# Second block: sine products and index logits left in PSUM, search rounds dealt over other units, pool copies and results put ahead of the index scores, the first two output units run in token halves

## The chip, the cores and the metric

The kernel runs on one core of a Trainium2 chip. The metric is the device time of one execution in microseconds (us), as the median of several runs. One more execution was taken by the hardware profiler; every duration below is from it.

## What is computed

The program runs two layers of a hybrid block (dilated attention, gated delta rule, gated feed-forward), then two layers of a second block. The change is made for the second block. Of one layer of it, with S = 512 tokens and a width of 1024:

```python
h = rms_norm_2(x, g_pre_mix[l])
proj = h @ w_in[l]
u_pool, q, k, v, iq, ik, iw = jnp.split(proj, SPLIT_POINTS, axis=-1)
q, k, iq, ik = (rope_partial(t, positions, 16) for t in (q, k, iq, ik))
# pool_mixer: window means of 2, 4, 8, 16 tokens minus u, times w_pool (4 groups of 128 channels)
a_out = pool_mixer(u_pool, w_pool[l], pool_scale[l])
# dsa_attention: which keys a query may look at
logits = jnp.einsum('bqhd,bsd->bqhs', iqb, ik32) * (IDX_DIM ** -0.5)
score = jnp.einsum('bqh,bqhs->bqs', iwb, jax.nn.relu(logits))     # 8 index heads
top_val, top_idx = lax.top_k(score, topk)                         # topk = 128
# softmax attention over the chosen keys, 8 heads of 64
b_out = dsa_attention(q, k, v, iq, ik, iw, topk)
mix = jnp.concatenate([a_out, b_out], axis=-1) @ w_out[l]
x = x + rms_norm_2(mix, g_post_mix[l])
f = jnp.square(jax.nn.relu(rms_norm_2(x, g_pre_ffn[l]) @ w_ff1[l])) @ w_ff2[l]
x = x + rms_norm_2(f, g_post_ffn[l])
```

## The kernel before, in words

Activations lie channel by token: a tile has 128 channels on the partitions and 512 tokens along the free axis. A **unit** is one tile of 128 output channels of a projection. TensorE (PE) makes it with 8 steps over the 1024 input channels (`unit`, L1869), and each step is three matmuls, because weights and activations are split into a high and a low fp32r part: high by high, low weight by high, high by low activation. For each unit SyncE loads 512 KB of weights (`load`, L705), ScalarE (ACT) makes the high part (`w_high`, L945), GpSimd (POOL) the low part by a subtraction (`w_low`, L761). Units alternate between two PSUM accumulators; a unit may start when the unit two before it has been copied out (`acc_free`).

Nothing is scheduled at run time. Each engine has its own list of instructions, written out in the order of the Python loops, and engines meet at semaphores; an engine whose next instruction waits holds up everything behind it. In the second block the loop over `u` from 0 to 21 gives that order for all engines:

- Units 0 to 4 are the index key and the index queries; 5 to 8 the four pool groups; 9 to 17 (without 11) queries and keys; 18 to 21 the values. "Unit" 11 (`WPOOL`) is the pool's own small product (`pool_mix`, L2045 to L2047).
- For rotated units ACT copies the accumulator to `turn2_in` (`turn_input`, L1032), PE multiplies by a permutation (`turn`, L2008) into `SC[j % 2]`, VectorE (DVE) multiplies by the sine (L1427), POOL multiplies the copy by the cosine (L901), DVE adds the two (L1431). `j` counts the turned units. The values are transposed instead (L2012), and DVE scales them out of PSUM into `v` (L1435).
- The pool units are scaled by DVE into `pu` (`unit_scaled`, L1416); this copy is what frees the accumulator. `pool_window` then adds shifted copies of `pu` (L1780, L1781), 1, 2, 3 or 4 times for g = 0 to 3, forms the mean minus `pu` (L1785 to L1789), and ACT and POOL split it (L986, L797). `pool_scaled` (L1768) reads the result of the small product from PSUM.
- The index logits are 16 **pairs** of matmuls (`index_logits`, L2000; two heads each, 128 to 512 keys wide), put between the last steps of units 6 to 10 and 12 by the table `IX_AT`. They alternate between two pairs of PSUM banks. ACT applies the ReLU into one of four SBUF buffers `ir` (L1261), DVE adds them up with the head's weight into `bias` (`index_score`, L1726, L1728).
- The search for the 128th largest score is 16 rounds for each of three query tiles (tile 1, 2 and 3, with 256, 384 and 512 keys). A round takes the 8 largest (L1742) and strikes them out (L1745); at the end of a tile `bias` becomes a mask (L1750). `TOP_AT` gives the rounds of each `u`, `TOP_STEPS` those that run within the attention.

Two places in DVE's loop over `u` set what follows (before):

```python
for y in (2 * pair + h for pair in IX_AT.get(u + 1, ()) for h in range(2)):
    index_score(w, y)
j = turn_of(1, u)
if j is not None:
    turn_finish(w, j)
elif u != WPOOL:
    pool_window(w, u - POOL_U)      # begins with unit_scaled
```

The attention (`attention`) has 35 slots; slot n makes scores (L2099), which DVE adds to `bias` (L1449), ACT exponentiates (L1041), PE transposes (L2111) and multiplies by `v` (L2124). Between them PE runs the 32 steps of the first half of the output product, whose input is the pool's result (`half_step` with `second` 0, L2069 to L2071). The second half needs the attention's result. It comes in four pieces of 128 tokens; each goes through ACT (L1056), DVE (L1467), ACT (L986) and POOL (L797) before PE may read it. After slot 34 PE runs 8 output units of 4 steps of 3 matmuls (`half_step` with `second` 1, the same lines).

## Time and profile before

| | us |
|---|---|
| median of 3 runs | 2866.94 |
| lowest, highest | 2864.83, 2867.55 |
| the profiled execution | 2872.96 |
| its span, first to last instruction | 2871.2 |
| PE busy in it | 2730.1 (95%) |
| second block, first layer: first unit to the end of the output product | 1554 to 1830 |
| the same of its second layer | 2214 to 2486 |

Times inside the span are counted from its start. "PE" rows are matmuls; their ends are modelled and overlap, so the distance from one start to the next is what a matmul costs. Numbers in square brackets behind a row are the idle time of the engine just before it, and who ended it. The granted clock of a stretch is 1.00 at 2.4 GHz and 0.50 at 1.2 GHz.

### The profile page before, as it was taken

To read this page: it belongs to the slowest core of one execution; us is meant where nothing else is said; L and a number is where in the kernel's file an instruction comes from. 1 tells how busy PE (TensorE), PEld (TensorE's weight loads), DVE (VectorE), ACT (ScalarE), POOL (GpSimd) and SP (SyncE) were. 2 spreads that over 40 slices of the span, in tenths; PEclk is the share of its full clock that TensorE was granted. 3 is DMA by queue.
4 is the path that set the end of the run, shared out by engine and by line. 5 is a ranking of instruction groups with operands and counts; after the bars stand their busy time and mean duration, and the time that the engine had idled before them with its cause. 6 is when DMAs were issued, how large, how long until landed. Compare 5 with 4: busy or idle time off the path is not lost.

```text
span 2871.2 us, 43482 instructions
## 1 busy us (share of the span) xinstructions
PE 2730.1 (95%) x15240; PEld 2153.9 (75%) x15240; DVE 1138.9 (40%) x2246; ACT 1111.2 (39%) x1846; POOL 1221.4 (43%) x630
## 2 busy tenths in 40 slices
PE   9998999999999989999999888899999898899997
PEld 7767778888776777788887566788887575688886
DVE  4555445440255553544303774410113675510012
ACT  4454244443335533444423325432323234542331
POOL 3313135554432222355544351364653451264553
PEclk9999999999999999999999999999999999999998
DMA  3211022222221101222232120122222121122222
GB/s 136 76 45 38 9 67 95 95 100 100 101 76 59 52 17 31 77 98 95 95 106 80 66 74 23 52 102 95 95 95 79 64 74 38 52 88 95 96 95 94
DMA packets 62871, 217.22 MB, mean 76 GB/s; under 512 B 6576, under 2 KB 6704, under 8 KB 62480
## 3 DMA queue, kind: packets, MB, share of 16 engines
q1 hardware_dynamic: 62416, 214.28, 21.9%
q8 instruction: 87, 1.43, 0.2%
q0 software_dynamic: 320, 1.12, 0.2%
q14 instruction: 48, 0.39, 0.0%
HBM read 213.28 MB, written 2.10 MB: 75 GB/s over the span
## 4 chain that ended last, share of the span: by engine, by line
PE 85%; DVE 7%; ACT 3%; issue 2%; DVEq 1%; POOL 1%; ACTq 0%; POOLq 0%
PE bank L1869 59%; PE bank L1919 3%; PE bank L2217 3%; PE bank L2069 2%; PE bank L2071 2%; PE bank L2070 2%; PE bank L1931 2%; PE bank L2124 1%; PE bank L2099 1%; PE bank L2111 1%; PE bank L2008 1%; POOL wL L761 1%; PE bank L2034 1%; PE bank L1896 1%; DVE bias L1728 1%
## 5 line engine op out<-in xcount | busy, mean ns | idle before, releaser
L761 POOL TENSOR_TENSOR wL<-raw,wH 128x1024 fp32r<-128x1024 f32 x371 | 903.3, 2435 | 1187.8 <-ACT wH L945 1187.5
L1869 PE MATMUL bank<-hH,wH 128*128 128x512 f32 x1680 | 688.9, 410 | 24.4 <-DVE pu L1416 16.3
L1869 PE MATMUL bank<-hH,wL 128*128 128x512 f32 x1680 | 658.9, 392 | 0.0
L1869 PE MATMUL bank<-hL,wH 128*128 128x512 f32 x1680 | 658.7, 392 | 0.0
L945 ACT ACTIVATE wH<-raw 128x1024 fp32r<-128x1024 f32 x371 | 392.1, 1057 | 519.2 <-PE bank L1869 489.4
L1869 PEld LDWEIGHTS bank<-hH,wH 128*128 128x128 f32 x1680 | 317.8, 189 | 124.1 <-issue 30.4
L1869 PEld LDWEIGHTS bank<-hH,wL 128*128 128x128 f32 x1680 | 318.3, 189 | 69.9 <-issue 9.8
L1869 PEld LDWEIGHTS bank<-hL,wH 128*128 128x128 f32 x1680 | 317.6, 189 | 67.9
L1869 PE MATMUL bank<-hidH,wH 128*128 128x512 f32 x864 | 337.3, 390 | 0.0
L1869 PE MATMUL bank<-hidH,wL 128*128 128x512 f32 x864 | 336.6, 390 | 0.0
L1869 PE MATMUL bank<-hidL,wH 128*128 128x512 f32 x864 | 336.6, 390 | 0.0
L1827 DVE SCALAR_TENSOR_TENSOR relu<-bank,rstd 128x512 f32<-128x512 f32 x64 | 44.1, 691 | 458.8 <-PE bank L1869 449.6
L1869 PEld LDWEIGHTS bank<-hidH,wH 128*128 128x128 f32 x864 | 162.2, 188 | 36.0 <-issue 1.6
L1869 PEld LDWEIGHTS bank<-hidL,wH 128*128 128x128 f32 x864 | 162.3, 188 | 33.8
L1869 PEld LDWEIGHTS bank<-hidH,wL 128*128 128x128 f32 x864 | 162.3, 188 | 32.9
L797 POOL TENSOR_TENSOR hidL<-piece,hidH 128x512 f32 (+1 forms) x108 | 139.8, 1295 | 99.4 <-ACT hidH L986 81.7
L1698 DVE SCALAR_TENSOR_TENSOR mT<-bank,par,mT 128x511 f32<-128x511 f32 (+1 forms) x176 | 131.9, 750 | 117.3 <-ACT mT L1223 103.2
L1041 ACT ACTIVATE sc<-sc,st 128x128 f32<-128x128 f32 (+3 forms) x128 | 71.7, 561 | 139.1 <-DVEq L1452 138.8
L1694 DVE TENSOR_TENSOR bank<-bank,rstd 128x512 f32<-128x512 f32 x88 | 61.5, 699 | 117.9 <-PE bank L1869 110.0
L2069 PE MATMUL bank<-hH,wH 128*128 128x512 f32 x192 | 78.8, 410 | 8.6 <-POOL hL L797 7.0
L990 ACT ACTIVATE sq<-mT 128x512 f32<-128x512 f32 x48 | 30.3, 632 | 131.0 <-DVE mT L1841 76.1
L1369 DVE TENSOR_TENSOR rstd<-rstd,sq 128x512 f32<-128x512 f32 x20 | 17.1, 855 | 150.3 <-ACT sq L990 150.3
(362 smaller groups left out, 3822.9 us busy)
## 6 DMA issues: line engine op xcount, KB each, us to landing
raw<-w_dram SPq DMA_DIRECT2D x398, 512.0 KB, 3.3
x<-x_dram SPq DMA_DIRECT2D x4, 512.0 KB, 9.4
out_dram<-x SPq DMA_DIRECT2D x1, 2048.0 KB, 6.2
const<-const_dram SPq DMA_DIRECT2D x1, 1229.0 KB, 12.8
par_next<-par_dram POOLq DMA_DIRECT2D x5, 168.0 KB, 3.6
qkT<-pos_dram POOLq DMA_DIRECT2D x1, 256.0 KB, 7.1
const<-const_dram SPq DMA_DIRECT2D x1, 131.0 KB, 2.2
```

Of the source, the lines that this page charges most:

```text
L761: pool.tensor_tensor(wL[:, s, :], raw[:, s, :], wH[:, s, :].bitcast(F32), ALU.subtract).then_inc(w_lo.sem, 1)
L797: pool.tensor_tensor(dst, shape(src), hi.bitcast(F32), ALU.subtract).then_inc(piece_lo.sem, 1)
L945: act.activation(wH[:, s, :], raw[:, s, :], ACT.Copy).then_inc(w_hi.sem, 1)
L1041: act.activation(sc[:, n % 2, 0:wd], sc[:, n % 2, 0:wd], ACT.Exp, bias=st[:, MN + n % 4:MN + n % 4 + 1], scale=-1.0, accum_out=st[:, SUM + ...
L1694: dve.tensor_tensor(banks[s][:, :], banks[s][:, :], rstd[:, :], ALU.mult).then_inc(acc_scaled.sem, 1)
L1698: last = dve.scalar_tensor_tensor(buf[:, lag:S], banks[s][:, 0:S - lag], prmd(w, "fconv", i * 12 + 6 * q + 3 * s + 2 - lag), buf[:, lag:S] ...
L1869: mm = pe.matmul((out or ACC[bk])[:, :], wt[:, c:c + P], rhs, start=first and k == 0 and j == 0, stop=last and k == tiles - 1 and j == 2)
L1919: pe.matmul(out[u][:, :], wt[:, k * P:k * P + P], hH[:, k, :], start=k == 0 and j == 0, stop=False)
L1931: mm = pe.matmul(out[u][:, :], three[u][0][:, k * P:k * P + P], hL[:, k, :], start=False, stop=k == KD - 1)
L2069: pe.matmul(out[:, :], wH[:, p % 2, c:c + P], high, start=k == 0, stop=False)
L2070: pe.matmul(out[:, :], wL[:, p % 2, c:c + P], high, start=False, stop=False)
L2217: mm = pe.matmul(o, *two, start=True, stop=True)
```

## The change

- `turn_finish`: the product with the sine is written back into the PSUM bank it was read from, in both blocks; the addition then reads PSUM and SBUF.
- `index_score` reads the logits from PSUM, where ACT's ReLU now leaves them. `ix_used` (DVE has read them) takes the place of `ix_relu` (ACT has copied them) in the waits of `index_logits` and `pool_mix`; the buffers `ir` and ACT's wait for them go.
- The last shifted addition of `pool_window` goes to the PSUM bank `SC[1]`; turn 5, the next to use that bank, waits until the fourth window is done.
- In DVE's loop `unit_scaled` and, at `WPOOL`, `pool_scaled` stand ahead of the index scores.
- The rounds are dealt anew: at `u` = 10 one for tiles 1 and 2; at 11 two for all three; at 12 to 20 one for all three, with one more for tile 1 at 13 to 16 and one more for tile 2 at 18 to 20; none at 21. Tile 2's last round runs in slot 1, five of tile 3 in slots 3 to 11 (six before).
- The last two transposes of values go to the banks `OA` and `TRO`, and slot 0 waits for turns 0 to 14 alone; slot 4 waits for all 17.
- The output units 0 and 1 of the second half run in two parts, tokens 0 to 255 and 256 to 511. The first part waits for two of the four attention pieces, the second for all.

```diff
@@ -184,16 +184,18 @@
 assert _y == 16
 
 
-TOP_AT, TOP_STEPS, _r, _r3 = {}, {}, 0, 0
-for _u in range(10, IN2):
-    _n, _n3 = 1 + (_u >= 18), int(_u >= 12)
-    TOP_AT[_u] = [[(1, r), (2, r)] + [(3, q) for q in range(_r3, _r3 + _n3)][r - _r:r - _r + 1]
-                  for r in range(_r, _r + _n)]
-    _r += _n
-    _r3 += _n3
-assert _r == TOPK // 8
-for _i, _q in enumerate(range(_r3, TOPK // 8)):
-    TOP_STEPS[2 * _i + 1] = [(3, _q)]
+TOP_AT = {10: [[1, 2]], 11: [[1, 2, 3], [1, 2, 3]]}
+for _u in range(12, IN2 - 1):
+    TOP_AT[_u] = [[1, 2, 3]] + ([[1]] if 13 <= _u < 17 else [[2]] if _u >= 18 else [])
+TOP_STEPS = {1: [[2]], 3: [[3]], 5: [[3]], 7: [[3]], 9: [[3]], 11: [[3]]}
+_done = {1: 0, 2: 0, 3: 0}
+for _table in (TOP_AT, TOP_STEPS):
+    for _u in sorted(_table):
+        for _c, _tiles in enumerate(_table[_u]):
+            _table[_u][_c] = [(i, _done[i] + _tiles[:n].count(i)) for n, i in enumerate(_tiles)]
+            for _i in _tiles:
+                _done[_i] += 1
+assert set(_done.values()) == {TOPK // 8}
 
 
 FILL, _f = [], 0
@@ -420,6 +422,10 @@
 
         SIDE = (bank[5], bank[6])
 
+        def turned_bank(b, j):
+
+            return (OA, TRO)[j - 15] if b and j >= 15 else SC[j % 2]
+
         def cst(name, a=0, b=None):
             o, n = CAT[name]
             return const[:, o + a:o + (n if b is None else b)]
...
@@ -1257,8 +1263,7 @@
                     for y in (2 * pair + h for pair in IX_AT.get(u, ()) for h in range(2)):
                         wd = P * (y // 8 + 1)
                         act.wait_ge(ix_done.sem, ix_done.at(w, y + 1))
-                        act.wait_ge(ix_used.sem, ix_used.at(w, y - 3))
-                        act.activation(ir[:, y % 4, 0:wd], index_bank(y)[:, 0:wd], ACT.Relu,
+                        act.activation(index_bank(y)[:, 0:wd], index_bank(y)[:, 0:wd], ACT.Relu,
                                        scale=HD ** -0.5).then_inc(ix_relu.sem, 1)
                     j = turn_of(1, u)
                     if j is not None:
@@ -1417,14 +1422,15 @@
 
             def turn_finish(w, j):
 
-                t1, t2 = ATT[w.b][3][:, 0, :], ATT[w.b][3][:, 1, :]
+                t2 = ATT[w.b][3][:, 1, :]
                 cos, sin = rope_r(w.b)
                 dve.wait_ge(turned.sem, turned.at(w, j + 1))
                 if j < N_ROT[w.b]:
                     if w.b:
                         t2 = pt2[:, j % 2, :]
                         dve.wait_ge(cos_done.sem, cos_done.at(w, j + 1))
-                    dve.tensor_tensor(t1, SC[j % 2][:, :], sin, ALU.mult)
+                    t1 = SC[j % 2][:, :]
+                    dve.tensor_tensor(t1, t1, sin, ALU.mult)
                     if w.b == 0:
                         dve.tensor_tensor(t2, turn_src(w.b, j), cos, ALU.mult)
                     dve.drain()
...
@@ -1720,7 +1726,7 @@
             def index_score(w, y):
 
                 i, h = y // 8, y % 8
-                score, r = bias_of(1, i), ir[:, y % 4, 0:P * (i + 1)]
+                score, r = bias_of(1, i), index_bank(y)[:, 0:P * (i + 1)]
                 dve.wait_ge(ix_relu.sem, ix_relu.at(w, y + 1))
                 if h == 0:
                     dve.tensor_scalar(score, r, iw[:, i, 0:1], None, ALU.mult).then_inc(ix_used.sem, 1)
@@ -1772,11 +1778,9 @@
 
                 win = 2 << g
                 u = pu[:, g % 2, :]
-                unit_scaled(w, POOL_U + g, u, acc_free[(POOL_U + g) % 2].sem)
-                dve.drain()
                 src = u
                 for step in range(g + 1):
-                    lag, dst = 1 << step, sc2[:, step % 2, :]
+                    lag, dst = 1 << step, sc2[:, step % 2, :] if step < g else SC[1][:, :]
                     dve.tensor_tensor(dst[:, lag:S], src[:, lag:S], src[:, 0:S - lag], ALU.add)
                     dve.tensor_copy(dst[:, 0:lag], src[:, 0:lag])
                     dve.drain()
@@ -1798,22 +1802,28 @@
                         copy_gates(w)
                     if u == 2:
                         gate_scale(w)
+                    j = turn_of(1, u)
+                    if j is None and u != WPOOL:
+                        unit_scaled(w, u, pu[:, (u - POOL_U) % 2, :], acc_free[u % 2].sem)
+                        dve.drain()
+                    if u == WPOOL:
+                        for g in (0, 1):
+                            pool_scaled(w, g)
                     for y in (2 * pair + h for pair in IX_AT.get(u + 1, ()) for h in range(2)):
                         index_score(w, y)
-                    j = turn_of(1, u)
                     if j is not None:
                         turn_finish(w, j)
                     elif u != WPOOL:
                         pool_window(w, u - POOL_U)
-                    if u in (WPOOL, WPOOL + 1):
-                        for g in (0, 1) if u == WPOOL else (2, 3):
+                    if u == WPOOL + 1:
+                        for g in (2, 3):
                             pool_scaled(w, g)
                     for rounds in TOP_AT.get(u, ()):
                         top_round(rounds)
                 for n in range(SLOTS):
                     attention(w, n)
-                    if n in TOP_STEPS:
-                        top_round(TOP_STEPS[n])
+                    for rounds in TOP_STEPS.get(n, ()):
+                        top_round(rounds)
                 sum_output(w, 0, lambda h: add_half(w, h))
                 residual(w, 0, "post", (w, 1))
                 dve.wait_ge(rstd_ready.sem, rstd_ready.at(w, 2))
@@ -1993,7 +2003,7 @@
                 if pair == 0:
                     pe.wait_ge(turn_done.sem, turn_done.at(w, 5))
                 if pair >= 2:
-                    pe.wait_ge(ix_relu.sem, ix_relu.at(w, 2 * pair - 2 * (pair < 15)))
+                    pe.wait_ge(ix_used.sem, ix_used.at(w, 2 * pair - 2 * (pair < 15)))
                 i = pair // 4
                 for y in (2 * pair, 2 * pair + 1):
                     p0, f = y % 2 * HD, y % 8 // 2
@@ -2001,15 +2011,19 @@
                               ikT[p0:p0 + HD, 0:P * (i + 1)], start=True, stop=True).then_inc(ix_done.sem, 1)
 
             def turn(w, j):
-                src = turn_src(w.b, j)
+                src, to = turn_src(w.b, j), turned_bank(w.b, j)
                 bk, a = acc_of(w, unit_of_turn(w.b, j))
                 pe.wait_ge(acc_free[bk].sem, acc_free[bk].at(w, a + 1))
+                if w.b and j == POOL_U:
+                    pe.wait_ge(piece_ready.sem, piece_ready.at(w, N_PD2 + 4))
+                if w.b and j == 15:
+                    pe.wait_ge(ix_used.sem, ix_used.at(w, 32))
                 if j < N_ROT[w.b]:
-                    pe.matmul(SC[j % 2][:, :], cst("turn2" if w.b else "turn1"), src, start=True,
+                    pe.matmul(to[:, :], cst("turn2" if w.b else "turn1"), src, start=True,
                               stop=True).then_inc(turned.sem, 1)
                 else:
                     for t in range(NT):
-                        tr = pe.transpose(SC[j % 2][:, t * P:t * P + P], src[:, t * P:t * P + P], ident)
+                        tr = pe.transpose(to[:, t * P:t * P + P], src[:, t * P:t * P + P], ident)
                     tr.then_inc(turned.sem, 1)
 
             def narrow(w):
...
@@ -2047,7 +2061,7 @@
                 pe.matmul(MIX[g % 2][:, :], pwH[:, c:c + P], pdL[:, g, :], start=False,
                           stop=True).then_inc(unit_done.sem if g == 1 else pool_done.sem, 1)
 
-            def half_step(w, h, k, second):
+            def half_step(w, h, k, second, part=None):
 
                 p, (bk, a) = HALF_OF[w.b][second] + h // 2, half_at(w.b, h, second)
                 out = half_bank(w.b, h, second)
@@ -2057,7 +2071,8 @@
                     pe.wait_ge(acc_free[bk].sem, acc_free[bk].at(w, a))
                 if h == 0 and w.b:
                     if k == 0:
-                        pe.wait_ge(piece_lo.sem, piece_lo.at(w, (N_ATT2 if second else N_PY2) + 4))
+                        pieces = (N_ATT2 if second else N_PY2) + (4 if part is None else 2 + 2 * part)
+                        pe.wait_ge(piece_lo.sem, piece_lo.at(w, pieces))
                 elif h == 0 and k == 0:
                     pe.wait_ge(piece_lo.sem, piece_lo.at(w, N_DN1 + NT if second else N_ATT1 + 4))
                 c = h % 2 * 512 + k * P
@@ -2066,10 +2081,11 @@
                 else:
                     r = k + 4 * second
                     high, low = hH[:, r, :], hL[:, r, :]
-                pe.matmul(out[:, :], wH[:, p % 2, c:c + P], high, start=k == 0, stop=False)
-                pe.matmul(out[:, :], wL[:, p % 2, c:c + P], high, start=False, stop=False)
-                mm = pe.matmul(out[:, :], wH[:, p % 2, c:c + P], low, start=False, stop=k == 3)
-                if k == 3:
+                cols = slice(0, S) if part is None else slice(S // 2 * part, S // 2 * part + S // 2)
+                pe.matmul(out[:, cols], wH[:, p % 2, c:c + P], high[:, cols], start=k == 0, stop=False)
+                pe.matmul(out[:, cols], wL[:, p % 2, c:c + P], high[:, cols], start=False, stop=False)
+                mm = pe.matmul(out[:, cols], wH[:, p % 2, c:c + P], low[:, cols], start=False, stop=k == 3)
+                if k == 3 and part != 0:
                     mm.then_inc(unit_done.sem if h % 2 else half_done.sem, 1)
 
             def gate_step(w, h, k):
@@ -2091,7 +2107,9 @@
                 pt = PTS[w.b]
 
                 if n == 0:
-                    pe.wait_ge(turn_done.sem, turn_done.at(w, (12, 17)[w.b]))
+                    pe.wait_ge(turn_done.sem, turn_done.at(w, (12, 15)[w.b]))
+                if n == 4 and w.b:
+                    pe.wait_ge(turn_done.sem, turn_done.at(w, 17))
                 if n < 32 and n % 2 == 0:
                     pe.wait_ge(sc_read.sem, sc_read.at(w, n))
                     f, i, _ = att_step(n)
@@ -2348,7 +2366,11 @@
                     attention(w, n, FILL[n])
                     if n < 16:
                         keep_warm(STAT, 1)
-                for h in range(KD):
+                for part in range(2):
+                    for h in range(2):
+                        for k in range(4):
+                            half_step(w, h, k, 1, part)
+                for h in range(2, KD):
                     for k in range(4):
                         half_step(w, h, k, 1)
                 output_sum(w, 0)
```

DVE, units 5 to 7 of a layer of the second block (in the middle of the loop over `u`); `pu` is the scaled pool unit, `bias` the scores, `sc` an SBUF buffer, `bank` any PSUM bank. Before:

```order
L1726 TENSOR_SCALAR bias<-ir,iw 128x128
L1728 SCALAR_TENSOR_TENSOR bias<-ir,iw,bias 128x128 x3
L1416 TENSOR_TENSOR pu<-bank,rstd 128x512
L1780 TENSOR_TENSOR sc<-pu 128x511
L1781 COPY sc<-pu 128x1
L1785 TENSOR_TENSOR sc<-sc,const 128x2
L1787 SCALAR_TENSOR_TENSOR piece<-sc,pu 128x512
L1789 TENSOR_TENSOR piece<-sc,pu 128x2
L1728 SCALAR_TENSOR_TENSOR bias<-ir,iw,bias 128x128 x4
```

and now:

```order
L1421 TENSOR_TENSOR pu<-bank,rstd 128x512
L1732 TENSOR_SCALAR bias<-bank,iw 128x128
L1734 SCALAR_TENSOR_TENSOR bias<-bank,iw,bias 128x128 x3
L1784 TENSOR_TENSOR bank<-pu 128x511
L1785 COPY bank<-pu 128x1
L1789 TENSOR_TENSOR sc<-bank,const 128x2
L1791 SCALAR_TENSOR_TENSOR piece<-bank,pu 128x512
L1793 TENSOR_TENSOR piece<-sc,pu 128x2
L1421 TENSOR_TENSOR pu<-bank,rstd 128x512
L1734 SCALAR_TENSOR_TENSOR bias<-bank,iw,bias 128x128 x4
```

The copy that frees the accumulator moved ahead of the scores, and most two-operand instructions now read one operand from a bank.

DVE, from the values of unit 20 to the first attention slot. Before:

```order
L1435 TENSOR_TENSOR v<-bank,rtok 128x4x128
L1742 MAX top<-bias 128x8 x3
L1745 MATCH_REPLACE bias<-top,bias 128x256
L1745 MATCH_REPLACE bias<-top,bias 128x384
L1745 MATCH_REPLACE bias<-top,bias 128x512
L1742 MAX top<-bias 128x8 x2
L1745 MATCH_REPLACE bias<-top,bias 128x256
L1745 MATCH_REPLACE bias<-top,bias 128x384
L1750 TENSOR_SCALAR bias<-bias 128x256
L1752 MEMSET bias 64x64
L1750 TENSOR_SCALAR bias<-bias 128x384
L1752 MEMSET bias 64x64
```

(the last `v` and the rounds of `u` = 21; those of `u` = 20 are the same without the masks), and now from the values of unit 20:

```order
L1441 TENSOR_TENSOR v<-bank,rtok 128x4x128
L1748 MAX top<-bias 128x8 x3
L1751 MATCH_REPLACE bias<-top,bias 128x256
L1751 MATCH_REPLACE bias<-top,bias 128x384
L1751 MATCH_REPLACE bias<-top,bias 128x512
L1756 TENSOR_SCALAR bias<-bias 128x256
L1758 MEMSET bias 64x64
L1748 MAX top<-bias 128x8
L1751 MATCH_REPLACE bias<-top,bias 128x384
L1441 TENSOR_TENSOR v<-bank,rtok 128x4x128
L1454 MEMSET st 128x1
L1455 ISA sc,st<-bank,bias 128x128
```

The last values are followed by the first slot directly; rounds remain only behind the values of unit 20.

PE, where the attention ends and the second half of the output product begins. Before:

```order
L2131 MATMUL bank<-const,st 64x128 x2
L2069 MATMUL bank<-hH,wH 128x512
L2070 MATMUL bank<-hH,wL 128x512
L2071 MATMUL bank<-hL,wH 128x512
L2069 MATMUL bank<-hH,wH 128x512
```

and now:

```order
L2149 MATMUL bank<-const,st 64x128 x2
L2085 MATMUL bank<-hH,wH 128x256
L2086 MATMUL bank<-hH,wL 128x256
L2087 MATMUL bank<-hL,wH 128x256
L2085 MATMUL bank<-hH,wH 128x256
```

24 matmuls of 512 columns became 48 of 256; the order of units 2 to 7 is as it was.

## Rows read from the trace of the kernel before

**Rows 1.** The profile's page: busy time, and the chain that ended last, by engine.
```profile
PE 2730.1 (95%) x15240; PEld 2153.9 (75%) x15240; DVE 1138.9 (40%) x2246; ACT 1111.2 (39%) x1846; POOL 1221.4 (43%) x630
...
PE 85%; DVE 7%; ACT 3%; issue 2%; DVEq 1%; POOL 1%; ACTq 0%; POOLq 0%
```
**Rows 2.** PE's waits, 1560 to 1840: us in total, times, longest.
```profile
PE bank L1869 <- DVE pu L1416: 8.6, 4, 3.9
PE bank L2099 <- DVE v L1435: 6.0, 1, 6.0
PE bank L2069 <- POOL hL L797: 3.5, 1, 3.5
...
PE bank L2045 <- DVE piece L1768: 2.6, 1, 2.6
PE bank L1869 <- POOL wL L761: 1.0, 1, 1.0
```
**Rows 3.** The same waits in the second layer, 2220 to 2500.
```profile
PE bank L1869 <- DVE pu L1416: 7.7, 4, 2.5
```
**Rows 4.** Stages, 1602 to 1812: PE, PEld, DVE, ACT, POOL busy, granted clock, DMA share, GB/s.
```profile
1604.00:1608.00 4.00, 3.50 (x9) 2.77 (x10) 3.76 (x7) 0.00 (x0) 2.19 (x1) 0.57 0.16 54
1806.00:1809.00 3.00, 2.81 (x7) 2.23 (x8) 0.00 (x0) 0.10 (x1) 0.14 (x1) 0.50 0.00 0
```
**Rows 5.** DVE and POOL in order of time, around 1604: start, us.
```profile
1603.76 0.69 DVE L1416 TENSOR_TENSOR pu<-bank,rstd 128x512 f32<-128x512 f32 x1
1604.54 2.20 DVE L1780 TENSOR_TENSOR sc<-pu 128x511 f32<-128x511 f32 x1
1603.83 2.36 POOL L761 TENSOR_TENSOR wL<-raw,wH 128x1024 fp32r<-128x1024 f32 x1 [3.20 <-ACT wH L945]
```
**Rows 6.** DVE by line and shape, 1565 to 1830: busy us, mean ns.
```profile
L1431 DVE TENSOR_TENSOR kT<-sc,pt 128x512 f32<-128x512 f32 x4 | 2.8, 692 | 0.3
L1427 DVE TENSOR_TENSOR sc<-bank,rope_r 128x512 f32<-128x512 f32 x13 | 9.0, 692 | 26.3 <-PE bank L2008 24.7 <-POOL pt L901 1.2 <-issue 0.3
```
**Rows 7.** Index logits, ReLUs and scores: PE, ACT and DVE in order of time.
```profile
1635.47 1.13 PE L2000 MATMUL bank<-ikT,iqT 64*128 64x512 f32 x4
...
1637.42 1.13 PE L2000 MATMUL bank<-ikT,iqT 64*128 64x512 f32 x4
1638.58 1.08 ACT L1261 ACTIVATE ir<-bank 128x512 f32<-128x512 f32 x2 [0.87 <-PE bank L2000]
1639.21 1.59 DVE L1728 SCALAR_TENSOR_TENSOR bias<-ir,iw,bias 128x512 f32<-128x512 f32 x2 [0.62 <-ACT ir L1261]
```
**Rows 8.** The fourth pool window, DVE in order of time.
```profile
1628.81 0.80 DVE L1780 TENSOR_TENSOR sc<-pu 128x511 f32<-128x511 f32 x1
...
1633.12 0.18 DVE L1789 TENSOR_TENSOR piece<-sc,pu 128x16 f32<-128x16 f32 x1
```
**Rows 9.** The turn from projection to attention: DVE and PE in order of time.
```profile
1713.89 0.69 DVE L1435 TENSOR_TENSOR v<-bank,rtok 128x512 f32<-128x512 f32 x1
...
1717.80 0.89 DVE L1742 MAX8 top<-bias 128x8 f32<-128x256 f32 x2
...
1719.85 0.69 DVE L1435 TENSOR_TENSOR v<-bank,rtok 128x512 f32<-128x512 f32 x1
1728.05 0.48 PE L2111 MATMUL bank<-const,sc 128*128 128x128 f32 x1 [2.98 <-ACT sc L1041]
```
**Rows 10.** The end of the attention: PE in order of time, and the chain at 1561.
```profile
1802.31 0.40 PE L2131 MATMUL bank<-const,st 128*64 128x128 f32 x4
1806.19 0.80 PE L2069 MATMUL bank<-hH,wH 128*128 128x512 f32 x1 [3.48 <-POOL hL L797]
1813.16 0.39 PE L2069 MATMUL bank<-hH,wH 128*128 128x512 f32 x1
...
1815.20 0.39 PE L2069 MATMUL bank<-hH,wH 128*128 128x512 f32 x1
...
1561.61 0.89 PE bank L1903 x8
```

8 lines of the change are left out of this document (4 added, 4 removed).

## The prediction

> **What bounds the kernel now.** The page comes first: PE is busy for 95% of the span, and the chain that ended last lies on PE for 85% and on DVE for 7% [rows 1]. The matmuls stay the same but for the last units, so only two things can be won: PE's idle time, and matmuls that run at half the granted clock. The waits of PE, stage by stage, give the first. In the first of the two layers PE waits four times, 8.6 us in all, for `unit_scaled` to free an accumulator, 6.0 for the last values before the attention, 3.5 for the low part of the attention's result, 2.6 for `pool_scaled` and 1.0 for weights [rows 2]. The second layer loses 7.7 instead of 8.6 in the first place [rows 3] and the same elsewhere. The table of stretches gives the second: behind a long wait the granted clock is mostly 0.5 and comes back some 3 us later (0.57 as a mean over 4 us at 1604, 0.50 over 3 us at 1806) [rows 4]. At half clock for 3.2 us, PE does what takes 1.6 us, so such a stretch costs 1.6. The first layer has three in the index and pool stage, after the second and the fourth wait for `unit_scaled` and after that for `pool_scaled`; the second layer has two.
>
> Index and pool stage before, waits and cold stretches: 8.6 + 2.6 + 1.0 + 3 x 1.6 = 17.0 in the first layer, 7.7 + 3.6 + 2 x 1.6 = 14.5 in the second.
>
> **Part 1: operands in PSUM.** The rows in order of time show why DVE is late. `unit_scaled`, from a bank, took 0.69 beside POOL's `w_low`, but the window's first addition, with both operands in SBUF, took 2.20, until POOL's 2.36 us subtraction was over (1603.83 + 2.36 = 1606.19; DVE ended at 1606.74) [rows 5]. With one operand in a bank the length is 0.69 with or without POOL: L1427 has 692 ns over 13 of them, equal to the 692 of L1431's `kT`, which reads SBUF twice and was not blocked [rows 6]. So `turn_finish`'s addition and the window's end are no longer held up (1.5 us at most each). I cost the edits themselves at nothing on DVE, since 692 = 692. **A rule against it:** the Trainium skill, "VectorE: DVE Perf Modes", section on the trn2 errata, gives an instruction a fixed part of 120 cycles with PSUM against 58 in SBUF. By that some 60 instructions per layer would be 0.065 us longer each, an estimate from that page of 3.9 us of DVE a layer, of which at most half would lie on a path: 3.9 us later in the two layers, 2841.5 in place of the 2837.6 below. The trace doesn't bear it out, as the equal means have just shown.
>
> **Part 2: results first, and the wait moved to `ix_used`.** Now `unit_scaled` and `pool_scaled` are ahead of the scores, so the waits of 8.6 and 2.6 in their old form go, but for what DVE has still to finish of the window before, which ends in time in every unit (below). But the logits stay in their bank until DVE has read them. ACT ends two ReLUs of 512 in 1.08, DVE two scores in 1.59 and 0.62 behind the first ReLU, so a pair is free 2.2 after it was made; pairs stand 1.95 apart [rows 7]. Two pairs are in flight, so this alone does not stop PE. What stops it is the window: the scores of unit u's pairs stand in DVE's list behind the window of unit u - 2. The fourth window takes 4.5 (1628.81 to 1633.30) [rows 8], 6.0 if POOL holds it up once as in [rows 5]; an addition and a copy less take 0.84 less. The third pair of a unit wants the first one's bank some 5.5 us after the third pair of the unit before; window and scores together need 4.5 to 6.0 + 0.6 + 1.6 = 6.7 to 8.2. That is a wait of 1.2 to 2.7 in unit 10; I take 2.3, nearer to the blocked end since POOL is busy in most of each unit, 2.1 in unit 9 and 1.2 in unit 8, whose windows and logits are shorter. Units 6 and 7 have windows of one step or none before them: nothing. `pool_mix` now waits until pair 13 is read (0.5 more than its weights, 0.6 kept), and pair 15 in unit 12, the only one that waits for its direct predecessor, waits for the two scores of pair 14: 1.9. Queued behind every such wait on PE is the rest of the unit; ACT and POOL then wait for PE, not PE for them. Sum: 1.2 + 2.1 + 2.3 + 0.5 + 0.6 + 1.9 = 8.6 us idle. Cold stretches: the waits are shorter than those of 3.9 and 2.6 which had one, about as long as the 1.9 at 1604.5 which had one, so I count two, 3.2 us. After: 11.8. **Gain: 17.0 - 11.8 = 5.2 in the first layer, 14.5 - 11.8 = 2.7 in the second, 7.9 in all.** Bounds: 0 (nothing but the place of the waits changes) and 23 (no third pair waits, `pool_mix` 1.1 and pair 15 1.9 stay, one cold stretch: 4.6 a layer, 12.4 + 9.9 = 22.3).
>
> Turn 5's new wait for the fourth window is a few us behind: that window now ends near the end of unit 10, turn 5 comes in unit 12's place. Nothing. The dealing of rounds up to u = 19 fills DVE to at most 5.96 - 2.05 + 1.2 = 5.1 us [rows 9] of PE's 24 x 0.2275 = 5.46 us a unit, so it costs nothing while DVE is not behind.
>
> **Part 3: the turn to the attention.** Before, the values of unit 20 began at 1713.89, those of unit 21 at 1719.85, and the first transposition of probabilities on PE at 1728.05, 8.20 later; a round for tiles 1 and 2 took 2.05 (1717.80 to 1719.85) [rows 9]. Now turns 15 and 16 go to other banks, so PE makes both at once and goes on to slot 0. DVE has between the two `v`: one round of three tiles, the mask of tile 1, a round of tile 2. That is 5.96 - 2.05 + 1.2 + 0.4 = 5.5, the 1.2 being the larger part of 2.05. But of the 8.20 behind the second `v`, all rounds go (5.96 - 0.6 = 5.35) and the mask of tile 1 (0.4) too. Net: 1713.89 + 5.5 + (8.20 - 5.35 - 0.4) = 1721.85, against 1728.05; 0.5 of this is tile 2's mask, which moves to slot 1: 1721.35. **Gain 6.7 a layer.** Late next: DVE's mask and round of tile 2 in slot 1, whose 1.7 us ACT and PE cover with slots and filling steps of the first half. Bounds: 5.5 if DVE is 1.2 late at unit 20, with 5.1 of 5.46 us a unit taken; 8 if slot 0 overlaps better. PE's clock is low in the first attention slots in both cases; nothing counted.
>
> **Part 4: the token halves.** PE ends the attention's last products at 1802.31 + 0.4, waits 3.48 for the low part and starts at 1806.19, at half clock until 1809; the first two units, 24 matmuls, last until 1813.16, 6.97 us, where 24 at the full rate of 0.2275 are 5.5 [rows 10]; the rate is 2.04 for the 9 from 1813.16 to 1815.20. Two of the four pieces have long been there (the query tiles take eight slots each, one tile after another, and a piece is one tile), so 24 half matmuls fill the wait, and 24 more remain behind it; the last two pieces are needed only then. The weights of these units are on the chip before (the wait names the pieces alone). The price of a matmul of 256 columns is not in the trace. Lower bound 0.111, which is 0.89/8 of L1903 with 128-column operands, close to half of 0.2275; upper bound 0.2275, if the weight load, 128x128 as before, sets it. I take 0.12, as PE runs on the columns and L1903's 0.111 contains a load each: 2.9 us in the wait, and 2.9 behind 1806.19 in place of 6.97, as the clock has no wait in front. **Gain 4.0 a layer.** With 0.2275: 24 in 5.5 from 1802.7 end 2.0 after the low part came, then 5.5 more: 1813.7, a loss of 0.6.
>
> **Sum.** 7.9 + 2 x 6.7 + 2 x 4.0 = 29.3, and -1 to 1 for the first block, where PE doesn't wait for `turn_finish`: nothing. The profiled execution would go from 2872.96 to 2843.7; the median of the runs is 6.0 below it, so 2866.9 - 29.3 = **2837.6**.
>
> **Rivals.** (a) *The waits only change place* in the index stage: 7.9 less, 2845.5. For: each third pair can wait, and DVE is busy 3.76 of 4 us there [rows 4]. Against: 8.6 and 2.6 had two causes, order and blocking, and both go. 15%. (b) *Half matmuls cost a full one*: 9.2 less, 2846.8. For: PE loads 128x128 weights for each. Against: L1903. 15%. (c) *The third pairs hardly wait*, because DVE is ahead where it was behind: 22.3 instead of 7.9, 2823.2. 12%. (d) *Slower:* a score that reads a bank and `bias` is itself blocked by POOL, 1.5 us (2.20 - 0.69) [rows 5] on each of the 14 pairs that wait: 21 us idle a layer, and with PE idle a third of the time 10 us of low clock; 31 + 3 in place of 15.8 (mean of the layers) is 18.2 lost, 10.7 gained in parts 3 and 4, 7.5 us a layer slower: 2881.9. It decides when the index stage loses over 10.7 a layer. Against it: L1427 at 692 ns reads SBUF and a bank beside POOL. 3%.
>
> **Chances.** The forecast 52%, (a) 15, (b) 15, (c) 12, (d) 3, (a) and (b) together 3 (2854.7). A measurement of this kernel can tell 0.2%, 5.7 us. Faster in all cases but (d) and a part of (a) with (b) and the lower bound of part 3 (2 x 1.2 more): faster 0.94, same 0.03, slower 0.03. The range goes from (c) to (a) with (b): 2822 to 2855.
>
> **What would show it.** Right: PE's waits for `pu` L1416 gone, new ones at the logits with `bias` as releaser, in units 8 to 10 and before pair 15, 1 to 2.5 us each; L1431's `qT` and `iqT` at 0.69 also beside POOL; L1780's last step likewise; the first probabilities' transposition about 8 us after unit 21; half matmuls 0.12 apart with no wait of 3.5. Wrong: DVE instructions from banks above 0.75 us; waits at the logits above 3 us; half matmuls 0.2 apart or a clock of 0.5 between them; rounds that run into slot 0.

## The result, and the profile after

| | before | changed |
|---|---|---|
| median of 4 runs, us | 2867.24 | 2833.45 |
| lowest, highest | 2864.83, 2867.61 | 2831.67, 2836.53 |
| ratio, 95% interval | | 0.9883 [0.9871, 0.9895] |
| the profiled execution | 2872.96 | 2831.67 |

The change takes 33.8 us off; 29.3 were forecast. The profiled executions lie 41.3 apart, since that of before is 6 above its median and that of the changed kernel 2 below its own. So the traces overstate the gain by some 8 us.

Both layers were cut into four stages. The cuts are rows of PE in order of time: the first logits; the first turn behind the second half of the pool's small product; the first transposition of probabilities; the start of the attention's last products with `st`; the first matmul of the output's square sum. Sums of both layers, us:

| kernel | index | to attention | attention | output | all four |
|---|---|---|---|---|---|
| before | 142.9 | 129.3 | 147.2 | 54.9 | 474.3 |
| changed | 126.6 | 115.6 | 144.3 | 48.6 | 435.1 |
| difference | 16.3 | 13.7 | 2.9 | 6.3 | 39.2 |

The page of the changed kernel, as in [rows 1]: PE is busy 16.6 us less with the same columns to multiply, which fits the granted clock (0.984 in the mean of the execution against 0.978: fewer columns run at half clock), and DVE's part of the chain is a point smaller.

```profile
PE 2713.5 (96%) x15288; PEld 2145.6 (76%) x15288; DVE 1106.0 (39%) x2246; ACT 1109.7 (39%) x1846; POOL 1211.0 (43%) x630
...
PE 86%; DVE 6%; ACT 3%; issue 2%; DVEq 2%; POOL 1%; DMA 0%; ACTq 0%; SPq 0%; POOLq 0%
```

PE's waits, changed kernel, 1555 to 1822 (us in total, times, longest), then the second layer, 2195 to 2470; they answer to [rows 2, 3]:

```profile
PE bank L2010 <- DVE bias L1734: 6.1, 4, 2.0
PE bank L2129 <- ACT sc L1047: 3.6, 1, 3.6
...
PE bank L2059 <- DVE bias L1734: 1.2, 1, 1.2
...
PE bank L2085 <- POOL hL L803: 0.4, 1, 0.4
```
```profile
PE bank L2010 <- DVE bias L1734: 7.4, 4, 2.8
```

The waits for `pu`, for `piece`, for `v` and of 3.5 for `hL` are gone. In their place PE waits at the logits (L2010), for DVE to have read a pair.

Stretches of the changed kernel, columns as in [rows 4]: after the short wait at 1607.5, after that of 2.04 at 1618.1, after the 3.56 before the first transposition, and the token halves.

```profile
1605.00:1609.00 4.00, 3.03 (x16) 1.76 (x16) 3.25 (x8) 2.37 (x7) 1.27 (x1) 1.00 0.36 123
1618.00:1622.00 4.00, 3.93 (x11) 2.56 (x12) 3.25 (x7) 1.97 (x4) 0.00 (x0) 0.58 0.00 0
1711.00:1714.00 3.00, 3.00 (x12) 2.16 (x11) 2.04 (x9) 0.91 (x5) 0.00 (x0) 0.50 0.00 0
1782.00:1788.00 6.00, 5.57 (x52) 5.19 (x49) 0.86 (x2) 2.51 (x3) 1.28 (x1) 1.00 0.29 86
```

The stage with the halves, PE in order of time, answers to [rows 10]. The last product of the attention at 1782.19 is followed by half matmuls at once; they start 0.12 apart, the last of the first part at 1785.37, and the wait for the last pieces is 0.43. The granted clock is 1.00 over the whole stretch.

```profile
1782.19 0.39 PE L2149 MATMUL bank<-const,st 128*64 128x128 f32 x4
1782.51 0.39 PE L2085 MATMUL bank<-hH,wH 128*128 128x256 f32 x1
...
1785.25 0.28 PE L2086 MATMUL bank<-hH,wL 128*128 128x256 f32 x1
1785.37 0.28 PE L2087 MATMUL bank<-hL,wH 128*128 128x256 f32 x1
1786.09 0.39 PE L2085 MATMUL bank<-hH,wH 128*128 128x256 f32 x1 [0.43 <-POOL hL L803]
```

DVE by line and shape answers to [rows 6]: first a row of before (1565 to 1830), then the changed kernel's (1560 to 1800).

```profile
L1431 DVE TENSOR_TENSOR iqT<-sc,pt 128x512 f32<-128x512 f32 x4 | 8.0, 2001 | 0.3
```
```profile
L1433 DVE TENSOR_TENSOR bank<-bank,rope_r 128x512 f32<-128x512 f32 x13 | 9.1, 700 | 18.7 <-PE bank L2022 16.0 <-POOL pt L907 1.9 <-issue 0.3
L1437 DVE TENSOR_TENSOR iqT<-bank,pt 128x512 f32<-128x512 f32 x4 | 2.8, 692 | 0.3
L1784 DVE TENSOR_TENSOR bank<-sc 128x510 f32<-128x510 f32 x1 | 2.7, 2668 | 0.1
```

The addition behind the sine product of the index queries went from 2.0 us in the mean to 692 ns. The window's last step is not protected by its result in PSUM: that of the second window still reads SBUF twice, and took 2.67 beside a subtraction of POOL that ran from 1601.34 to 1603.73.

### The profile page after: what moved, and what is told of

Its sections match the earlier page's. It is cut to its first block, busy times and chain, and to the rows that moved or that the text cites. A ratio compares the mean times of both kernels' runs of the same rounds, so it can differ in the third digit from the quotient of the medians.

```text
span 2829.9 us, 43533 instructions
## 1 busy us (share of the span) xinstructions
PE 2713.5 (96%) x15288; PEld 2145.6 (76%) x15288; DVE 1106.0 (39%) x2246; ACT 1109.7 (39%) x1846; POOL 1211.0 (43%) x630
## 4 chain that ended last, share of the span: by engine, by line
PE 86%; DVE 6%; ACT 3%; issue 2%; DVEq 2%; POOL 1%; DMA 0%; ACTq 0%; SPq 0%; POOLq 0%
PE bank L1879 60%; PE bank L1929 3%; PE bank L2235 3%; PE bank L2085 2%; PE bank L2087 2%; PE bank L2086 2%; PE bank L1941 2%; PE bank L2142 1%; PE bank L2117 1%; PE bank L2129 1%; PE bank L2022 1%; POOL wL L767 1%; PE bank L2048 1%; PE bank L1906 1%; PE bank L1913 1%
## 5 line engine op out<-in xcount | busy, mean ns | idle before, releaser
L1879 PE MATMUL bank<-hH,wH 128*128 128x512 f32 x1680 | 685.0, 408 | 6.1 <-POOL wL L767 6.0
L803 POOL TENSOR_TENSOR hidL<-piece,hidH 128x512 f32 (+1 forms) x108 | 139.9, 1296 | 100.6 <-ACT hidH L992 81.6
L2085 PE MATMUL bank<-hH,wH 128*128 128x512 f32 (+1 forms) x208 | 81.0, 389 | 2.5 <-POOL wL L767 1.4
L2086 PE MATMUL bank<-hH,wL 128*128 128x512 f32 (+1 forms) x208 | 77.8, 374 | 0.0
```

The costliest lines, as they stand in the source:

```text
L803: pool.tensor_tensor(dst, shape(src), hi.bitcast(F32), ALU.subtract).then_inc(piece_lo.sem, 1)
L1879: mm = pe.matmul((out or ACC[bk])[:, :], wt[:, c:c + P], rhs, start=first and k == 0 and j == 0, stop=last and k == tiles - 1 and j == 2)
L2085: pe.matmul(out[:, cols], wH[:, p % 2, c:c + P], high[:, cols], start=k == 0, stop=False)
L2086: pe.matmul(out[:, cols], wL[:, p % 2, c:c + P], high[:, cols], start=False, stop=False)
```

## The experiments

Eleven kernels ran, each beside the kernel before. The table has the stages, both layers together, from one profile each. In these stages a stretch at half clock is 3.41 us long in every profile, or twice that, so one more or less moves an entry by 1.7 us. The last column is the median of before minus that of the kernel, by runs on the same chip; of the changed kernel it is 33.8. The expectations name times as on the chip of the result, where the kernel before took 2867.24. On the chips of the experiments it took 2869.22 (e1 to e4), 2871.18 (e5 to e8) and 2871.14 (e9 to e11), so the gain decides and not the time. The 95% intervals reach 0.0016 to 0.0022 to either side of the ratio, 5 to 6 us.

| kernel | index | to attention | attention | output | all four | gain |
|---|---|---|---|---|---|---|
| e1 no halves | 125.8 | 115.6 | 144.5 | 56.6 | 442.5 | 27.5 |
| e2 old rounds and banks | 127.7 | 129.3 | 142.9 | 48.4 | 448.3 | 21.7 |
| e3 order only | 127.0 | 129.3 | 144.6 | 58.0 | 458.9 | 14.1 |
| e4 operands, order undone | 139.9 | 115.6 | 148.5 | 48.6 | 452.7 | 16.8 |
| e5 no PSUM operands | 127.0 | 118.4 | 146.4 | 48.5 | 440.2 | 33.8 |
| e6 window first | 132.0 | 115.6 | 145.7 | 48.5 | 441.9 | 33.7 |
| e7 that, logits in SBUF | 115.0 | 115.6 | 144.3 | 48.7 | 423.6 | 49.6 |
| e8 new rounds, old banks | 127.0 | 123.8 | 141.4 | 48.4 | 440.7 | 32.4 |
| e9 split late | 130.9 | 115.6 | 142.9 | 48.4 | 437.8 | 35.6 |
| e10 that, logits in SBUF | 123.8 | 115.6 | 147.2 | 48.6 | 435.1 | 36.2 |
| e11 e7, rounds in slots | 116.6 | 108.2 | 142.7 | 48.4 | 415.9 | 56.6 |

**e1, the token halves alone undone.**

```diff
-                for part in range(2):
-                    for h in range(2):
-                        for k in range(4):
-                            half_step(w, h, k, 1, part)
-                for h in range(2, KD):
+                for h in range(KD):
```

> The changed kernel without the token halves: output units 0 and 1 of the second half run whole, behind the wait for all four pieces. Theory (the halves fill PE's 3.5 us wait and keep the granted clock up): the wait of 3.5 us for the low part comes back in both layers, 2.4 us a layer with the clock at full behind it and 4.0 where it falls to half: 5 to 8 us more than the changed kernel, about 2840. Rival (PE's gain at this place came from the clock in one execution only): no difference that can be measured, 2833 to 2836.

2841.71, ratio 0.9901 [0.9885, 0.9918]: 6.3 less gain, as the theory has it. Its output stage is 8.0 longer in the trace, and the waits of its first layer hold the row of before again:

```profile
PE bank L2085 <- POOL hL L803: 3.5, 1, 3.5
```

In the traces the halves are worth 4.0 us a layer where the clock would fall behind the wait, 2.4 where it would not, as in the second layer of before.

**e2, rounds and banks of before.** `TOP_AT`, `TOP_STEPS`, `turned_bank` and slot 0's wait as before.

> The changed kernel with the search rounds dealt as before, the last two values' transposes in the banks of before, and slot 0 behind all 17 turns. Theory (the turn to the attention is the rounds that stand between unit 20 and slot 0 on DVE): PE's 6 us wait before slot 0 comes back, 6.8 us a layer, 2847. Rival (the index stage leaves DVE ahead now, and rounds would be done anyway): under 6 us in all, below 2839.

2847.51, ratio 0.9925 [0.9908, 0.9941]: 12.1 less gain. The stage to the attention is 129.3, to a tenth that of before, and 13.7 above the changed kernel: 6.9 a layer. The attention behind it is 1.4 shorter in both layers together, so the net is nearer to the 12.1 of the medians.

**e3, the order alone, on the kernel before.** (`pool_window` no longer begins with `unit_scaled`, and `pool_scaled` of the first two groups isn't called behind the scores.)

```diff
+                    j = turn_of(1, u)
+                    if j is None and u != WPOOL:
+                        unit_scaled(w, u, pu[:, (u - POOL_U) % 2, :], acc_free[u % 2].sem)
+                        dve.drain()
+                    if u == WPOOL:
+                        for g in (0, 1):
+                            pool_scaled(w, g)
                     for y in (2 * pair + h for pair in IX_AT.get(u + 1, ()) for h in range(2)):
                         index_score(w, y)
```

> The kernel before with one edit: unit_scaled and pool_scaled stand ahead of the index scores in DVE's list; operands, logits buffers, rounds, banks and halves as before. Theory (order and bank operands are both needed): the copies that free accumulators come at once, but the windows are still blocked by POOL beside them and the ReLUs wait for one of four SBUF buffers, so 3 to 5 of the 8 us a layer come: 2857 to 2861. Rival 1 (the order gives the whole of the index stage): 16 us, 2851 or less, with no wait over 1 us left there. Rival 2 (the operands give it): 2865 to 2868.

2855.08, ratio 0.9951 [0.9935, 0.9968]. The gain of 14.1 lies between my theory (6 to 10) and rival 1 (16), nearer to the rival, and the index stage decides for it: 127.0 against 126.6 of the changed kernel, with every operand where it was before. (The output stage, which this edit doesn't touch, is 3.1 longer than before: its second layer had 6.8 us at half clock, where before had none.) The rival's "no wait over 1 us" was wrong; PE waits at the logits here too, for ACT (first layer):

```profile
PE bank L2004 <- ACT ir L1261: 6.0, 4, 2.7
```

**e4, the changed kernel with that order undone.** The same edit backwards.

> The changed kernel with one edit undone: unit_scaled and pool_scaled stand behind the index scores again. Theory (both are needed): PE waits for pu again, 1 to 2 us in four places, and at the logits: 6 us a layer more than the changed kernel, about 2845. Rival 1 (the order gives the whole): 8 us a layer more, 2850. Rival 2 (the operands give it): within 3 us of the changed kernel, 2834 to 2836.

2852.43, ratio 0.9941 [0.9924, 0.9957]: 17.0 less gain, as rival 1 has it. The index stage is 139.9, 3.0 below before. PE waits for DVE again (first layer):

```profile
PE bank L1875 <- DVE pu L1421: 6.0, 4, 1.8
...
PE bank L2055 <- DVE piece L1774: 2.6, 1, 2.6
PE bank L2006 <- DVE bias L1734: 2.0, 2, 1.4
```

So of the 16.3 us the order gives 15.9 alone; all the rest of the change gives 3.0 without it and 0.4 beside it. Even the 3.0 is hardly the operands' own: PE's waits in the stage are only 0.9 shorter than before in both layers together (23.3 against 24.2), and the stage has two stretches at half clock fewer. No run parts the order into its two halves, `unit_scaled` and `pool_scaled`.

**e5, no PSUM operands in the changed kernel.**

> The changed kernel without its PSUM operands: sine product, last window step and the ReLU's logits go to SBUF as before, with the four buffers and their waits; order, rounds, banks of the last values and halves as in the change. Theory after the last runs (the order alone shortens the index stage, operands nothing): as the changed kernel within 2 us, 2832 to 2836, index stage 63 to 64 us. Rival (bank operands save DVE the time that POOL blocks it, and this shows once the rest is in place): 3 to 6 us more, 2837 to 2840, with waits for weights or for DVE that the changed kernel lacks.

2837.36, ratio 0.9887 [0.9869, 0.9906], against 0.9883 of the change: the same gain, 33.8, though the time by itself would fall into the rival's range. The trace shows one place that the rival foresaw, small: the stage to the attention is 1.4 a layer longer. DVE's four additions for `qT` take 1208 ns in the mean here, 692 in the change, it has no idle time to speak of in front of the values (0.3 us instead of 2.7), and slot 0 comes later (PE waits 4.82 instead of 3.56 before the first transposition):

```profile
1713.91 0.48 PE L2129 MATMUL bank<-const,sc 128*128 128x128 f32 x1 [4.82 <-ACT sc L1047]
```

**e6 and e7, the window first.** In DVE's list a unit's window now follows `unit_scaled`, ahead of the next unit's scores; e7 also has the ReLU write to the four buffers `ir`, with the waits of before.

```diff
+                    if j is None and u != WPOOL:
+                        pool_window(w, u - POOL_U)
                     for y in (2 * pair + h for pair in IX_AT.get(u + 1, ()) for h in range(2)):
                         index_score(w, y)
                     if j is not None:
                         turn_finish(w, j)
-                    elif u != WPOOL:
-                        pool_window(w, u - POOL_U)
```

> The changed kernel with one more move in DVE's list: the pool window of a unit stands before the index scores of the next unit, right behind unit_scaled, not behind them. Theory (the third pair of units 8, 9 and 10 waits for scores that stand behind a window begun too late; DVE is idle at a unit's start, when the first pair isn't made yet): the three waits before third pairs, 4.6 us in the first layer and 5.8 in the second, go, and the cold stretch behind one of them: 10 to 13 us in all, 2821 to 2824. Rival 1 (the window then delays the scores of the first pair as much as it did before): within 3 us, 2831 to 2836. Rival 2 (scores late, and behind them unit_scaled: PE waits for pu again): slower by 5 us or more, 2838 upwards.

> As the run with the window first, but the ReLU writes the logits to four SBUF buffers as in the kernel before (sine product and window end stay in PSUM). Theory (where the logits lie costs nothing either way, since four buffers and four banks both hold two pairs): within 2 us of the run with the window first. Rival (freeing the bank at the ReLU takes away the waits before pool_mix and pair 15, 2.7 us a layer, and with the window first no buffer is short): 4 to 6 us faster than that run.

e6: 2837.52, ratio 0.9887 [0.9871, 0.9904], a gain of 33.7, so rival 1. e7: 2821.59, ratio 0.9831 [0.9812, 0.985], 15.9 better than e6, where 4 to 6 was the most that I had set down. PE's waits in the first layer, e6 above, e7 below:

```profile
PE bank L2010 <- DVE bias L1734: 7.4, 4, 2.6
```
```profile
PE bank L1880 <- POOL wL L767: 1.8, 1, 1.8
PE bank L2060 <- ACT ir L1267: 1.2, 1, 1.2
```

In e7 no third pair waits. A likely reason shows in ACT's rows of the changed kernel. ACT's list has the split of a window's result (`pdH`, L992) ahead of the next unit's ReLUs (L1266), and the split waits for the window:

```profile
1615.65 0.63 ACT L992 ACTIVATE pdH<-piece 128x512 fp32r<-128x512 f32 x1 [5.36 <-DVEq L1794]
1616.18 1.61 ACT L1266 ACTIVATE bank<-bank 128x384 f32<-128x384 f32 x4
```

The two pairs were made at 1612.48 and 1614.22; their ReLUs start at 1616.18, behind the split, and the third pair at 1618.07. With the window late, buffers in SBUF are of no use, since it is the ReLU that would free the bank, and it stands still: e3 and e5. With the window first and the logits in PSUM, ACT goes on, but the bank is held until DVE has done window and score: e6. Only both edits together give the gain; that much the runs show. Why is argued from the waits: a bank is free at the ReLU, and four pairs can be ahead of DVE's reading instead of two. No run had more buffers, and e10 below shows that ACT's standing still is not the whole of it.

**e8, the new rounds with the banks of before.**

> The changed kernel with the last two values' transposes in the score banks as before and slot 0 behind all 17 turns; rounds dealt as in the change. Theory (of the 6.8 us a layer at the turn to the attention the dealing of rounds is most: slot 0 now waits for the last v on DVE, 6 us behind unit 21, and its scores reach DVE some 1 us late): 1 to 1.5 us a layer more than the changed kernel, 2835.5 to 2836.5. Rival (both are needed, since DVE still has to do a round between the two values, and slot 0 waits for that): 4 us a layer or more, above 2841.

2838.80, ratio 0.99 [0.9878, 0.9922]. The stage to the attention is 4.1 a layer longer, the attention behind it 1.5 shorter (the clock falls during the wait and is back sooner). In the stage itself the rival holds; with the attention it is 2.6 a layer, and the medians' 1.4 us less gain in all can't be told from nothing. Of the 6.9 us of that stage the dealing of rounds alone brings 2.8, the banks 4.1 on top of it.

**e9 and e10, ACT's split behind the ReLUs**, DVE's order as in the change; e10 with the four buffers.

```diff
+                    if 1 < u - POOL_U <= 5:
+                        g = u - POOL_U - 2
+                        piece_high(w, N_PD2 + g, piece[:, g % 2, :], pdH[:, g, :])
                     if j is not None:
...
-                    if 0 < u - POOL_U <= 4:
-                        g = u - POOL_U - 1
-                        piece_high(w, N_PD2 + g, piece[:, g % 2, :], pdH[:, g, :])
```

> The changed kernel with one move in ACT's list: the high part of a pool window's result (pdH) is taken behind the next unit's ReLUs instead of ahead of them; DVE's order and the logits in PSUM as in the change. Theory (ACT's ReLUs stand behind the wait for the window, but DVE's scores stand behind that window too, so with the logits in PSUM a pair is held by DVE either way): waits before third pairs shorter by the 0.6 to 1.0 us that ReLU and split take, 2 to 4 us in all, 2829 to 2832. Rival (ACT's wait for the window is the whole cause of those waits): they go, 10 us, about 2823.

> The last edit, and the ReLU writes the logits to four SBUF buffers. Theory (a bank is then free at the ReLU, which now waits for no window, so four pairs can be ahead of DVE instead of two): the waits before third pairs in units 8 to 10 go or stay under 1 us, as in the run with window first and no logits in PSUM, 2821 to 2826. Rival 1 (what helped there was the window's place alone): 2832 to 2837. Rival 2 (scores that read two SBUF operands are blocked by POOL and eat it up): index stage no shorter than 62 us.

e9: 2835.58, ratio 0.9874 [0.9857, 0.989]. e10: 2834.97, ratio 0.9873 [0.9854, 0.9891]. Neither can be told from the changed kernel. In e9 PE waits at the logits longer than in the change, and no longer at `pool_mix` (7.1 us in the first layer against 6.1 and 1.2), so DVE holds the pairs either way. The 2 to 4 us don't show in the trace: the index stage is 4.3 longer, most of it half clock.

```profile
PE bank L2010 <- DVE bias L1734: 7.1, 4, 2.5
```

In e10 the waits before third pairs did go, and other waits came (first layer):

```profile
PE bank L1880 <- POOL wL L767: 2.3, 1, 2.3
PE bank L2023 <- DVEq L1795: 1.8, 1, 1.8
PE bank L1880 <- DVE pu L1422: 1.4, 1, 1.4
PE bank L2060 <- ACT ir L1267: 1.1, 1, 1.1
```

The second is turn 5, which waits for the fourth window, since that ends in its bank; I had costed this wait at nothing, and in the changed kernel it is nothing. By its time e10 is where rival 1 put it, not at my 2821 to 2826. Rival 2's sign is nearly there too (61.7 and 62.0 us a layer, scores blocked for 7 us a layer beyond what a score of their width takes otherwise), but e7 has 6.4 us of such blocking and 57.5 us. So releasing ACT and the banks is not enough: the window's place on DVE is a large part of what e7 gains (115.0 against 123.8).

**e11, the rounds of unit 20 in the attention's slots**, on top of e7.

```diff
+del TOP_AT[20]
-TOP_STEPS = {1: [[2]], 3: [[3]], 5: [[3]], 7: [[3]], 9: [[3]], 11: [[3]]}
+TOP_STEPS = {1: [[1]], 3: [[2]], 5: [[2]], 7: [[2]], 9: [[3]], 11: [[3]], 13: [[3]], 15: [[3]], 17: [[3]], 19: [[3]]}
```

> The run with the window first and no logits in PSUM, and the rounds of unit 20 dealt to the attention's slots: none behind unit 20, one for tile 1 in slot 1, tile 2 in slots 3, 5 and 7, tile 3 in slots 9 to 19. The first eight slots read tile 0, which isn't searched. Theory (slot 0 waits for DVE's rounds without need, and PE's wait of 3.6 us before the first transposition of probabilities puts the clock at half behind it): 3.5 us plus 1.7 of clock less in each layer, 10 us in all, 2811 to 2813. Rival 1 (the wait is the chain ACT and DVE need for a slot anyway): under 1 us a layer. Rival 2 (rounds in slots delay the attention's own DVE work): the attention 3 to 6 us longer, no gain.

2814.56, ratio 0.9803 [0.9787, 0.9819], 7.0 better than e7, where 10 were expected, and 22.8 better than the changed kernel. The wait before the first transposition and the half clock behind it are gone, 3.7 a layer up to that point. PE in order of time; the first row is slot 0's scores:

```profile
1702.77 0.49 PE L2119 MATMUL bank<-kT,qT 64*128 64x128 f32 x4
...
1705.60 0.27 PE L2131 MATMUL bank<-const,sc 128*128 128x128 f32 x1
```

Of the clock's 1.7 a layer only half arrived (142.7 against 144.3): the attention has two waits for ACT that e7 lacks, 0.41 and 1.32 us, near the last two rounds for tile 3, in slots 17 and 19. Rival 2's mechanism holds for that part; its "no gain" does not.

```profile
1744.50 0.52 PE L2131 MATMUL bank<-const,sc 128*128 128x128 f32 x3 [0.41 <-ACT pt L1057]
...
1750.65 0.52 PE L2131 MATMUL bank<-const,sc 128*128 128x128 f32 x3 [1.32 <-ACT turn_in L1057]
```

## Why the prediction was right, and where it was off

- **Forecast and result.** 2837.6 against 2833.45, in the range, and faster as forecast. That the two lie only 4.2 us apart is in part luck. One term, the index stage, was forecast 8.4 us too small by the traces, twice that distance; the attention, costed at nothing, adds 2.9 in them, and the halves and the turn together were 1.4 too large. With these the traces have 39.2 us in the four stages; the profiled execution of before ran 6 us above its median, and so 33.8 came out. The medians have the same pattern without the profiles: e4 puts the order at 17.0 us, e2 rounds and banks at 12.1 (13.4 forecast), e1 the halves at 6.3 (8.0 forecast).
- **Part 1, operands.** The forecast costed the edits at nothing on DVE, and saw their use in additions that POOL no longer blocks. The turns are as it says (iqT 692 ns). The window's end is not: one of its four last steps was blocked for 2.67 us. All this is worth little: e5 shows 1.4 us a layer in the trace and nothing that the medians tell. The largest effect on DVE was not counted and yet gives nothing: with the logits in SBUF POOL blocks scores too, 11.1 us in e5's first layer beyond what a score of their width takes otherwise, 0.0 in the change. PE's waits in the stage are 6.5 and 7.2 us even so, since in the one the bank is free at the ReLU and in the other only when DVE has read it.
- **The rule set aside.** The Trainium skill ("VectorE: DVE Perf Modes", the trn2 errata) gives a PSUM source 62 cycles more in the fixed part of an instruction, an estimate of 0.065 us. It was set aside on the equal means of 692 ns, and no row of this case bears it out. Instructions that read two tensors take the same from either (692 for the additions, 752 and 750 for the scores of 512). The four scores a layer that read one tensor (L1726 before, L1732 now) do take longer from PSUM, but by a share of the width and not by a fixed part: from SBUF 288, 353 and 485 ns for 128, 256 and 512 columns, from PSUM 350, 484 and 751. That is 0.51 and 1.04 ns a column, and a fixed part of 222 and 216 ns, an estimate from these rows. The difference at 128 columns, 0.062, is near the rule's 0.065 by chance. It costs 0.46 us a layer in these three; the one of 384 was blocked by POOL before (1173 ns) and takes 618 now.

```profile
L1726 DVE TENSOR_SCALAR bias<-ir,iw 128x512 f32<-128x512 f32 x1 | 0.5, 485 | 0.5 <-ACT ir L1261 0.5
L1726 DVE TENSOR_SCALAR bias<-ir,iw 128x128 f32<-128x128 f32 x1 | 0.3, 288 | 1.6 <-ACT ir L1261 1.6
```
```profile
L1732 DVE TENSOR_SCALAR bias<-bank,iw 128x512 f32<-128x512 f32 x1 | 0.8, 751 | 0.1
L1732 DVE TENSOR_SCALAR bias<-bank,iw 128x128 f32<-128x128 f32 x1 | 0.3, 350 | 2.6 <-ACT bank L1266 2.6
```

- **Part 2, the index stage: the term that was mis-sized.** Forecast 7.9, trace 16.3. "After: 11.8" was 9.0 in the first layer and 9.2 in the second. The waits of the first were 0.97, 2.04, 1.57, 1.16 and 1.50, 7.2 in all against 8.6 forecast; those of the second 7.5; and each layer had one stretch at half clock instead of two. Of the 8.4 us missed, some 3.0 are that clock, 2.5 the shorter waits, 1.2 the sum of before, which was 0.6 a layer short, and 1.7 lie in neither waits nor clock and stay unexplained. The waits came where they were put (third pairs of units 8, 9 and 10, `pool_mix`, pair 15), and in the first layer each within 0.75 us of the forecast; `pool_mix` no longer waited in the second layer. The working named window and scores on DVE as the cause of third pairs' waits. For the changed kernel that stands: with ACT's split moved out of the way the waits stay (e9). That ACT's ReLUs wait behind the split was missed; it matters only once the ReLU frees the bank (e5, e10). The text also gave the gain to order and operands together; e3 and e4 give it to the order.
- **Part 3.** Forecast 6.7 a layer, measured 6.86 in the trace (64.67 to 57.81 in the first layer); e2 takes that stage back to the tenth, and costs 12.1 us by the medians for both layers. The path was the one forecast: the last values came 5.82 behind those before (5.5 in the working) and the first transposition 1.54 behind them (1.95), 8.0 after unit 21 (1702.81 to 1710.81) as "about 8 us" says.
- **Part 4.** Forecast 4.0 a layer. Measured 3.95 in the first and 2.4 in the second. The forecast read its rows in the first layer alone, and took its half clock for both; the second layer's stage was at full clock before. A half matmul took the 0.12 that was taken; rival (b) falls.
- **Attention.** Forecast 0, trace 2.9 in the first layer and 0.0 in the second. In the first layer the profiled execution of before had two stretches at half clock there, some 6 and 3 us long, the changed kernel's one of 3; in the second both had 6 to 7 us of it. Which waits bring such a stretch differs from one profile to the next, and this may be part of the 8 us by which the traces overstate the medians.
- **Rivals.** (a) and (c) fall: the waits changed place and shrank to half. (d) falls: the blocking that it puts on a score from PSUM hits scores with both operands in SBUF (e5: 1198 and 1303 ns in the mean for 256 and 512 columns), and never one from PSUM (484 and 750).

```profile
L1734 DVE SCALAR_TENSOR_TENSOR bias<-ir,iw,bias 128x512 f32<-128x512 f32 x7 | 9.1, 1303 | 0.9 <-issue 0.5
...
L1734 DVE SCALAR_TENSOR_TENSOR bias<-ir,iw,bias 128x256 f32<-128x256 f32 x7 | 8.4, 1198 | 0.7 <-ACT ir L1267 0.2
```

## What to carry to other kernels

Where engines run lists written in advance, ask of each instruction that waits what stands behind it: moving the copies that free buffers ahead of other work was worth 14 to 17 us here, changing where operands lie nothing that the medians tell. An edit can be without effect until another stands beside it: window first alone gave nothing (e6), logits in SBUF alone nothing (e5, by which the sine products and window ends went to SBUF too), both 15.8 us (e7). So for each buffer list who frees it, and what that engine has queued ahead; here the ReLU waited for ACT's split, and the score for the window. Moving the split and freeing the bank at the ReLU took the waits before third pairs away and brought others (e10), so go on to the next engine of the chain before costing it. Work without a near deadline, such as the rounds for tiles that the first eight slots don't read, belongs behind the first work that PE waits for.
